# An encoder layer with routed experts: x laid out transposed by the host, router work reordered, one sum in DRAM

## The chip, the core and the metric

The kernel runs on one NeuronCore of a Trainium2 chip. Its engines are TensorE (PE, with PEld for the weight loads), VectorE (DVE), ScalarE (ACT), GpSimd (POOL) and SyncE (SP). SP and ACT issue plain DMAs. POOL issues the DMAs whose rows are named by an index table, and the accumulating ones, from its own queue. The metric is the device time of one execution in microseconds (us); less is better.

## The reference, cut to what matters

1024 tokens of width 1024 go through one layer. The first half is a projection (with a convolution, a pooling and an attention branch), an output projection, a residual sum and a layer norm. The second half sends each token to 8 of 64 experts and to one shared expert:

```python
x = layer_norm(DEEPNORM_ALPHA * x + mix, ln1_g[l], ln1_b[l])
scores = sigmoid((x @ w_router).astype(float32))
_, idx = lax.top_k(scores + router_bias, TOP_K)          # 8 of 64
gates = sel / sum(sel) * ROUTED_SCALE
def expert_block(acc, blk):                               # blocks of 128 rows of one expert
    tok, g, e = blk
    xb = x_pad[tok]
    h = silu(xb @ w_gate[e]) * (xb @ w_up[e])
    return acc.at[tok].add((h @ w_down[e]) * g[:, None]), None
shared = swiglu(xt, w_gate_sh, w_up_sh, w_down_sh)
x = layer_norm(DEEPNORM_ALPHA * x + routed + shared, ln2_g[l], ln2_b[l])
```

All matrix products but a few are made to nearly f32 precision from a high and a low part of both operands, as three products (`PRODS`).

## The kernel before, in words

**Start.** SP loads eight tiles of x, 128 tokens by 1024 channels each, into `xin` (line 370), the first weight block `wraw` after four of them (line 372), then mem and two more weight blocks. PE transposes every x tile (lines 1541 to 1545, the helper at 1536), ACT copies the transposes out of PSUM as the high part of `xT` (line 707), DVE subtracts to get the low part (line 1032). Then come the 20 projection jobs of `JOBS` in their order (line 1546), each with its weight block split by ACT (`split_hi`, line 700) and DVE (`split_lo`, line 1023). `gate0`, the transposes of mem, `a0` and `gate1` are the first on PE (line 1561 for the products). The gated product of `gate0` and `a0` (line 1132) starts the convolution on DVE (lines 1105 and 1109), which runs on through the later jobs.

**In front of the expert loop.** For each tile t of 128 tokens, PE runs the output projection, transposes the normalised tile x1 (line 1710), then runs the shared expert's gate and up products of tile t - 1 (line 1729) and the router logits of tile t (line 1716). DVE routes (line 1258), ranks (line 1236), and POOL scatters the (token, gate) pairs into `list_d`, 8 indirect DMAs per tile (line 598). After the last tile DVE and PE build the tables of work items (lines 1349 and 1769), the shared expert's rows are finished (down products, lines 1829 to 1847), and ACT writes them with plain DMAs into the second half of `sum_d` (`put_shared`, line 919). SP writes x1 into the first half (line 410). When all list scatters have landed, POOL loads the first index tables (line 669) and gathers the rows of the first item (line 639).

**The expert loop.** An item is 128 rows of one expert; there are 96. Per item PE transposes the gathered rows of the next item, transposes the hidden rows of the item before (line 1821), and runs gate and up (line 1790) and the down products of the item before (line 1808). ACT scales the result into `ysb[s]` (`y_out`, line 912) after the scatter that last read that buffer has landed (line 941), copies the high parts, and at an expert's first item also those of the next expert's three weight matrices (lines 899 and 837); DVE makes the low parts. SP streams each expert's three 1 MB matrices into eight slots (`load_expert`, line 434). POOL runs `fetch` in order: gather of an item two ahead (line 639), load of an index table (line 632), then `add_rows` (line 644), an accumulating scatter of a finished item into one of two DRAM sums, chosen by the item's parity, so that neighbouring scatters may be in flight together:

```python
def fetch(q, c):
    gather(q, c + 1)
    if not isinstance(q, int) or q * RING + c - 5 >= NT:
        g.wait_ge(s_yd[(c - 5) % 2], 16 * nth_put(q, c - 5))
    ...
    load_pairs(q, c + 3)
    if not isinstance(q, int) or q * RING + c - 3 >= NT:
        add_rows(q, c - 3)
```

**The end.** SP loads both sums (`load_early`, `load_late`, lines 503 to 516). Tiles 0 and 4 (`ADDED`) are added by DVE (line 1516), the others by PE with an identity matrix (line 1865). ACT takes the moments of six tiles (lines 993 to 1003), DVE those of tiles 0 and 4 (line 1504), POOL the reciprocal root (line 690), DVE normalises every tile in order (lines 1492 to 1499), SP writes it out (line 519).

## Time and profile before

| what | value |
|---|---|
| time, median of 3 runs | 1371.61 us (1370.96 to 1372.6) |
| the profiled execution's own time | 1372.02 us |
| its span, first to last instruction | 1370.4 us |
| mean granted TensorE clock | 0.976 of full speed |
| PE busy, share of the span | 1302.6 us, 95% |
| DVE, ACT, POOL busy | 955.1, 795.3, 486.4 us |

The span is what the trace shows; 1.6 us of the execution's time lie outside it. Rows of the trace give a start and a duration in us from the span's start, the engine, the line of the kernel, and in brackets the idle time ahead of an instruction and what ended it.

### The profile page before, as it was taken

The numbers are of one execution on the slowest core, as the hardware profiler recorded it, in microseconds if no ns is written. First come the engines' busy times: TensorE is split into PE (matmuls) and PEld (weight loads), VectorE is DVE, ScalarE is ACT, GpSimd is POOL, SyncE is SP. The second block draws the span as 40 slices with busy tenths as digits, with TensorE's granted clock in tenths as the row PEclk, the third lists the DMA queues.
The fourth block names the chain that finished last, engine by engine and source line by source line (L and its number), as shares of the span: only waits on it lengthen the run. The fifth ranks groups of instructions, "written<-read, shape, count | busy, mean of one in ns | idle before, by whom it ended". The sixth has DMA issues, their size and how long they took to land.

```text
span 1370.4 us, 25641 instructions
## 1 busy us (share of the span) xinstructions
PE 1302.6 (95%) x6331; PEld 1076.4 (79%) x6332; DVE 955.1 (70%) x1121; ACT 795.3 (58%) x1055; POOL 486.4 (35%) x440
## 2 busy tenths in 40 slices
PE   8989888999988999999999999999999999999966
PEld 6877676788867888888888888888888888788842
DVE  5799986876663968565787366557678679777736
ACT  4122276322344868575796466656678678677724
POOL 0000124366563343343343343334334344443322
PEclk9999989999998999999999999999999999999987
DMA  6022124222468998987999788869889899999657
GB/s 249 31 77 78 62 92 132 93 87 85 136 219 323 329 331 309 325 270 251 332 338 342 235 251 273 260 197 316 277 277 377 250 329 336 339 341 299 191 135 289
DMA packets 78065, 324.11 MB, mean 237 GB/s; under 512 B 22656, under 2 KB 24864, under 8 KB 52816
## 3 DMA queue, kind: packets, MB, share of 16 engines
q1 hardware_dynamic: 43152, 251.05, 48.8%
q0 software_dynamic: 33728, 68.47, 21.4%
q10 hardware_dynamic: 1152, 4.19, 0.8%
q8 instruction: 16, 0.26, 0.1%
q14 instruction: 17, 0.14, 0.0%
HBM read 290.51 MB, written 67.72 MB: 261 GB/s over the span
## 4 chain that ended last, share of the span: by engine, by line
PE 86%; DVE 6%; DMA 3%; issue 2%; ACT 2%; POOL 1%; SPq 0%; POOLq 0%; ACTq 0%; DVEq 0%
PE ps L1790 39%; PE ps L1808 19%; PE ps L1536 7%; PE ps L1657 6%; PE ps L1561 6%; PE ps L1736 2%; DVE cv L1109 2%; PE ps L1821 2%; POOL list_d L598 1%; PE ps L1648 1%; PE ps L1573 1%; DMA xin<-in_x 1%; PE ps L1566 1%; PE ps L1724 1%; DMA late__124<-sum_d 1%
## 5 line engine op out<-in xcount | busy, mean ns | idle before, releaser
L1790 PE MATMUL ps<-wgu,xTe 128*128 x2304 | 548.9, 394 | 2.5 <-ACT wgu L837 1.2
L1790 PEld LDWEIGHTS ps<-wgu,xTe 128*128 128x128 f32 x2304 | 425.7, 188 | 89.3 <-issue 4.3
L649 POOL DMA_INDIRECT sum_d<-ysb,idx x95 | 176.8, 1861 | 510.5 <-ACT ysb L914 403.4
L1808 PE MATMUL ps<-wdn,hT 128*128 (+1 forms) x1236 | 299.5, 391 | 0.0
L1407 DVE TENSOR_TENSOR wgu<-raw,wgu (+1 forms) x128 | 287.7, 2289 | 6.4 <-issue 3.1
L1808 PEld LDWEIGHTS ps<-wdn,hT 128*128 128x128 f32 x1236 | 232.6, 189 | 48.2
L837 ACT CAST wgu<-raw (+1 forms) x128 | 246.9, 1929 | 4.1 <-SPq L448 3.6
L1412 DVE TENSOR_TENSOR xTe<-ps,xTe 128x512 fp32r<-128x512 f32 x194 | 124.6, 684 | 141.9 <-ACT xTe L906 141.9
L914 ACT ACTIVATE ysb<-ps,idx 128x512 f32<-128x512 f32 x188 | 119.3, 686 | 122.3 <-PE ps L1808 122.3
L1407 DVE TENSOR_TENSOR wdn<-raw,wdn x64 | 146.7, 2293 | 59.5 <-ACT wdn L899 59.3
L639 POOL DMA_INDIRECT xg<-x_d,idx x99 | 112.4, 1135 | 44.7 <-issue 35.5
L899 ACT CAST wdn<-raw x64 | 124.9, 1952 | 0.0
L958 ACT ACTIVATE hs<-ps 128x256 f32<-128x256 f32 x96 | 36.9, 384 | 142.2 <-PE ps L1790 142.2
L906 ACT CAST xTe<-ps 128x512 fp32r<-128x512 f32 x194 | 104.3, 598 | 12.1 <-PE ps L1536 11.3
L1536 PE MATMUL ps<-ident,xg 128*128 128x128 f32 x776 | 101.3, 274 | 10.4 <-DMA xg<-x_d,idx 10.4
L1561 PE MATMUL ps<-xT,whl 128*128 128x512 f32 x480 | 110.1, 390 | 0.0
L1536 PEld LDWEIGHTS ps<-ident,xg 128*128 128x128 f32 x776 | 91.0, 141 | 23.4 <-DMA xg<-x_d,idx 10.8
L1561 PEld LDWEIGHTS ps<-xT,whl 128*128 128x128 f32 x480 | 89.9, 188 | 19.2 <-issue 0.4
L1441 DVE TENSOR_TENSOR hx<-hs,ps 128x256 f32<-128x256 f32 x96 | 40.1, 417 | 88.2 <-ACT hs L958 88.1
L598 POOL DMA_INDIRECT list_d<-tg,addr x64 | 76.7, 1199 | 54.9 <-DVEq L1256 38.3
L1657 PE MATMUL ps<-wo,mst 128*128 128x512 f32 x384 | 92.9, 400 | 0.4 <-issue 0.4
L1657 PEld LDWEIGHTS ps<-wo,mst 128*128 128x128 f32 x384 | 72.6, 192 | 15.8 <-issue 0.9
(229 smaller groups left out, 1161.6 us busy)
## 6 DMA issues: line engine op xcount, KB each, us to landing
raw<-in_w_gate SPq DMA_DIRECT2D x64, 1024.0 KB, 11.7
raw<-in_w_up SPq DMA_DIRECT2D x64, 1024.0 KB, 8.8
raw<-in_w_down SPq DMA_DIRECT2D x64, 1024.0 KB, 9.7
wraw<-in_w_in SPq DMA_DIRECT2D x10, 512.0 KB, 3.4
xin<-in_x SPq DMA_DIRECT2D x8, 512.0 KB, 7.8
wraw<-in_w_kv SPq DMA_DIRECT2D x8, 512.0 KB, 3.3
wor<-in_w_out SPq DMA_DIRECT2D x4, 1024.0 KB, 8.6
xres<-in_x SPq DMA_DIRECT2D x8, 512.0 KB, 4.5
```

The source lines that it names most:

```text
L639: g.indirect_dma_start(out=xg[:, c % 2], out_offset=None, in_=x1_d, in_offset=bass.IndirectOffsetOnAxis(ap=idx[:, c % RING, 0:1], axis=0), ...
L649: g.indirect_dma_start(out=sums, out_offset=bass.IndirectOffsetOnAxis(ap=idx[:, c % RING, c % 2:c % 2 + 1], axis=0), in_=ysb[:, c % 2], in ...
L837: nc.scalar.copy(wgu[:, v, 0, :, n * XD:(n + 1) * XD].rearrange("p a c n -> p (a c) n"), raw[:, bass.ds(slot_of(e, n), 1)].rearrange("p a ...
L899: nc.scalar.copy(wdn[:, v, 0].rearrange("p a c n -> p (a c) n"), raw[:, bass.ds(slot_of(e, 2), 1)].rearrange("p a (c n) -> p (a c) n", c=2 ...
L914: nc.scalar.activation(dst[:, b * 512:(b + 1) * 512], ps[:, bank + b, :], ACT.Copy, scale=scale).then_inc(s_y, 1)
L1407: V.tensor_tensor(dst, raw_, hi.bitcast(F), ALU.subtract).then_inc(done, 1)
L1412: last = V.tensor_tensor(xTe[:, s, 1, 4 * b:4 * b + 4], ps[:, b, :].rearrange("p (c n) -> p c n", c=4), xTe[:, s, 0, 4 * b:4 * b + 4].bitc ...
L1536: last = nc.tensor.transpose(ps[:, bank + c // 4, (c % 4) * 128:(c % 4 + 1) * 128], src[:, c * 128:(c + 1) * 128], ident[:])
L1561: last = mm(ps[:, b + h, :], wt[:, st, d], xT[:, mo, d, h * 512:(h + 1) * 512], start=(d == 0 and st == 0 and mo == 0), stop=(d == ND - 1 ...
L1657: last = mm(ps[:, project_bank(t, h), :], mixed(t)[:, st, c], wo[:, mo, c, h * 512:(h + 1) * 512], start=(first and c == blocks[0] and st ...
L1790: last = mm(ps[:, 2 + s, :], xTe[:, s, st, d], wgu[:, w, mo, d].rearrange("p a n -> p (a n)"), start=(d == 0 and st == 0 and mo == 0), sto ...
L1808: last = mm(ps[:, down_bank(i) + h, :], hT[:, s, st, c], wdn[:, w, mo, c, h * 512:(h + 1) * 512].rearrange("p a n -> p (a n)"), start=(c = ...
```

## The change

- The host also lays x out transposed (`xt`: two halves of 512 tokens, each in four pieces of 128 partitions by 1024). The kernel loads these pieces, ACT and DVE split them straight from SBUF, the 64 PE transposes go, and PE runs `gate0` and `a0` half by half. The transposes of mem follow behind `a0`.
- In front of the loop, logits move between two parts of the shared expert's products (`BEFORE`: after 4 of 8 blocks, at the last tile after 7), DVE routes before it multiplies the shared hidden rows, and the rank product of tile 6 moves ahead of the transposes of tile 7. The item tables are made by one matmul with a ones matrix over diagonals that DVE builds (`tdiag`).
- There is one `sum_d`. x1 is written into it, POOL adds the shared rows with accumulating DMAs (`add_shared`) in place of ACT's plain writes, and every expert scatter goes to it. Each scatter waits until the one ahead has landed. ACT waits for the adds of shared tiles 2 to 5 before it overwrites their SBUF rows with an expert's weights. SP holds expert 2's second load until the list scatters have landed (`s_seen`).
- At the end each tile of the one sum is loaded and used directly.

```diff
+BEFORE = (4,) * (NT - 1) + (7,)
-        sum_d = nc.dram_tensor("sum_d", [2, S, D], F, kind="Internal").ap()
+        sum_d = nc.dram_tensor("sum_d", [S, D], F, kind="Internal").ap()
# SP
-            for t in range(NT):
-                sp.dma_start(xin[:, t], a["x"][t]).then_inc(s_x[t], 16)
-                if t == 3:
-                    project_weights(0)
+            for h in range(2):
+                project_weights(h)
+                for c in range(4):
+                    sp.dma_start(xin[:, h, c], a["xt"][h, c]).then_inc(s_x[4 * h + c], 16)
+            project_weights(2)
...
                 if e0 == 2:
                     landed(e0, 0, rounds)
+                    sp.wait_ge(s_seen, 1)
...
             for t in range(NT):
-                if t >= 2:
-                    load_early(t, s_late[t])
-                load_late(t)
+                sp.dma_start(late_[:, t], sum_d[t * 128:(t + 1) * 128, :]).then_inc(s_late[t], 16)
# POOL
+            def add_shared(j):
+                g.wait_ge(s_y, 2 * j + 4)
+                landed = s_ysf if j < 2 else s_ysh
+                g.dma_start(sum_d[j * 128:(j + 1) * 128, :], shared_rows(j), accum_op=ALU.add).then_inc(landed[j % 2], 16)
+            add_shared(0)
+            add_shared(1)
             g.wait_ge(s_tabs, 1)
...
                 g.wait_ge(s_y, 2 * (q * RING + c) + 4)
+                if not isinstance(q, int) or q * RING + c > NT:
+                    g.wait_ge(s_yd[(c - 1) % 2], 16 * nth_put(q, c - 1))
...
             for r in range(RING):
                 fetch(1, r)
+                if r == 0:
+                    for j in range(2, NT - 2):
+                        add_shared(j)
+                elif r < 3:
+                    add_shared(NT - 3 + r)
# ACT
+            for h in range(2):
+                split_hi(h)
+                for c in range(4):
+                    act.wait_ge(s_x[4 * h + c], 16)
+                    nc.scalar.copy(xT[:, 0, 2 * c:2 * c + 2, h * 512:(h + 1) * 512],
+                                   xin[:, h, c].rearrange("p (a n) -> p a n", a=2)).then_inc(s_xhi, 1)
...
+                scores_of(t)
                 if t >= 1:
                     shared_silu(t - 1)
-                scores_of(t)
...
-                put_shared(u)
...
                 nxt = act.value_load(tab[0:1, 1, bass.ds(i, 1)], min_val=0, max_val=NE)
+                if known and i == NT:
+                    for parity in range(2):
+                        act.wait_ge(s_ysh[parity], 16 * 2)
# DVE
+            for h in range(2):
+                split_lo(h)
+                for c in range(4):
+                    v.wait_ge(s_xhi, 4 * h + c + 1)
...
+            route(NT - 1)
             shared_hidden(NT - 2)
-            route(NT - 1)
...
+                for b, n in ((0, 128), (1, TAB - 128)):
+                    step(V.tensor_tensor(tdiag[:, :, b * 128:b * 128 + n], ...
...
-            add(0)
             moments(0)
# PE
+            for h in range(2):
+                for j in range(2):
+                    if h == 0:
+                        pe.wait_ge(s_wlo, j + 1)
+                    for d in range(ND):
+                        if j == 0 and d % 2 == 0:
+                            pe.wait_ge(s_xlo, 4 * h + d // 2 + 1)
+                        for st, mo in PRODS:
+                            last = mm(ps[:, result(j) + h, :], whl[:, j, st, d], xT[:, mo, d, h * 512:(h + 1) * 512], ...
...
+                if t == NT - 1:
+                    ranks(t - 1)
                 x1_transposed(t)
+                if t >= 1:
+                    shared_gate_up(t - 1, range(BEFORE[t]))
                 if t == NT - 1:
                     hidden_transposed(0)
-                    ranks(t - 1)
+                logits(t)
                 if t >= 1:
-                    shared_gate_up(t - 1)
-                logits(t)
+                    shared_gate_up(t - 1, range(BEFORE[t], ND))
...
-            pe.wait_ge(s_early, 32)
-            add_part(1, early)
-            for t in summed:
...
-                add_part(t, late_).then_inc(s_pc, 1)
```

## Rows read from the trace of the kernel before

**Rows 1.** The page: the chain that ended last, by engine.
```profile
PE 86%; DVE 6%; DMA 3%; issue 2%; ACT 2%; POOL 1%; SPq 0%; POOLq 0%; ACTq 0%; DVEq 0%
```
**Rows 2.** Stretches: PE, PEld, DVE, ACT, POOL busy us; granted clock, DMA share, GB/s.
```profile
416.80:444.00 27.20, 27.14 (x129) 22.98 (x130) 12.46 (x14) 14.56 (x22) 6.20 (x7) 0.91 0.96 375
600.00:1100.00 500.00, 499.98 (x2476) 419.94 (x2475) 326.45 (x315) 336.03 (x423) 190.63 (x161) 1.00 0.88 285
1100.00:1292.00 192.00, 189.36 (x929) 157.81 (x929) 145.07 (x128) 141.38 (x166) 75.90 (x62) 1.00 0.94 316
```
**Rows 3.** The page's groups: line, engine, op, count, busy us, mean ns, idle before.
```profile
L899 ACT CAST wdn<-raw x64 | 124.9, 1952 | 0.0
L958 ACT ACTIVATE hs<-ps 128x256 f32<-128x256 f32 x96 | 36.9, 384 | 142.2 <-PE ps L1790 142.2
```
**Rows 4.** The chain in order of time (start us, us, what), 0 to 200 us.
```profile
16.91 10.93 PE ps L1561 x48
29.60 21.78 PE ps L1561 x96
```
**Rows 5.** The timeline of the start.
```profile
15.82 1.09 PE L1536 MATMUL ps<-ident,xin 128*128 128x128 f32 x8 [0.19 <-DMA xin<-in_x]
40.52 1.23 DVE L1132 TENSOR_TENSOR glu<-ps,glu 128x1024 f32<-128x1024 f32 x1 [9.13 <-PE ps L1561]
40.60 1.05 ACT L700 CAST whl<-wraw 128x1024 fp32r<-128x1024 f32 x1 [10.47 <-PE ps L1561]
```
**Rows 6.** The timeline in front of the loop.
```profile
373.23 1.93 ACT L892 CAST wdn<-wdnr 128x2048 fp32r<-128x2048 f32 x1
381.62 0.29 DVE L1261 TENSOR_REDUCE sb__96<-ps 128x64 f32<-128x128 f32 x1
416.86 1.97 PE L1536 MATMUL ps<-ident,xg 128*128 128x128 f32 x8 [10.39 <-DMA xg<-x_d,idx]
```
**Rows 7.** The chain in order of time, 200 to 430 us.
```profile
400.44 6.25 DMA list_d<-tg,addr
```
**Rows 8.** The timeline of the loop's first items.
```profile
419.68 1.03 POOL L639 DMA_INDIRECT xg<-x_d,idx  x1 [4.50 <-issue]
425.90 1.91 ACT L899 CAST wdn<-raw  x1
430.53 0.41 DVE L1441 TENSOR_TENSOR hx<-hs,ps 128x256 f32<-128x256 f32 x1
432.96 0.38 PE L1821 MATMUL ps<-ident,hx 128*128 128x128 f32 x2
```
**Rows 9.** All instructions of line 649, the scatters: the last row of that view.
```profile
DMA to landing us min/median/max: 4.6/10.3/12.3
```
**Rows 10.** The chain in order of time, 600 to 620 us: two items' first gate and up products.
```profile
600.91 5.47 PE ps L1790 x24
...
610.20 5.47 PE ps L1790 x24
```
**Rows 11.** DMA issues (count, KB, median us to landing): 583 to 585, 592.5 to 594.5, 440 to 560.
```profile
sum_d<-ysb,idx POOLq DMA_INDIRECT x1, 6.2
...
sum_d<-ysb,idx POOLq DMA_INDIRECT x1, 10.8
...
sum_d<-ysb,idx POOLq DMA_INDIRECT x13, 10.8
```
**Rows 12.** The timeline of the end.
```profile
1333.11 1.23 DVE L1516 TENSOR_TENSOR acc<-early,late__124 128x1024 f32<-128x1024 f32 x1 [11.95 <-DMA late__124<-sum_d]
1334.37 1.29 DVE L1504 BATCH_NORM_STATS2 stat<-acc 128x6 f32<-128x512 f32 x2
1336.01 1.27 DVE L1492 SCALAR_TENSOR_TENSOR acc<-acc,mv,g 128x1024 f32<-128x1024 f32 x1
1342.42 1.28 DVE L1496 SCALAR_TENSOR_TENSOR acc<-ps,lnst,g 128x1024 f32<-128x1024 f32 x1 [3.24 <-POOL rs L690]
1366.09 1.28 DVE L1499 SCALAR_TENSOR_TENSOR acc<-acc,rs,b 128x1024 f32<-128x1024 f32 x1
```

More of the change, by code:

```diff
@@ L409, in _ @@
                 sp.wait_ge(s_x1, t + 1)
-                for rows in (x1_d, xa_d):
+                for rows in (x1_d, sum_d):
                     sp.dma_start(rows[t * 128:(t + 1) * 128, :], xres[:, t % 2]).then_inc(s_x1w[t % 2], 16)
@@ L713, in _ @@
                     split_hi(17)
-                elif w in W_JOBS and W_JOBS.index(w) < 16:
+                elif w in W_JOBS and 0 < W_JOBS.index(w) < 16:
                     split_hi(W_JOBS.index(w) + 1)
@@ L940, in step_act @@
                 shared = known and i - 2 < NT
[L941 removed]
+                if known and i < NT + 2:
+                    act.wait_ge(s_ysf[s], 16)
+                elif known:
+                    act.wait_ge(s_ysh[s], 16 * (NT // 2 - 1))
+                else:
+                    act.wait_ge(s_yd[s], 16 * nth)
                 act.wait_ge(s_dn, i - 1)
                 y_out(ysb[:, s], 1.0 / ALPHA if shared else idx[:, bass.ds((i - 2) % RING, 1), 2:3].bitcast(F).rearrange("p a n -> p (a n)"))
[L944 to L945 removed]
                 item_hi(i + 1, 1 - s)
@@ L1096, in _ @@
                 both = ps[:, b:b + 2, :].rearrange("p a n -> p (a n)")
-                if w in W_JOBS and W_JOBS.index(w) < 17:
+                if w in W_JOBS and 0 < W_JOBS.index(w) < 17:
                     split_lo(W_JOBS.index(w) + 1)
@@ L1540, in _ @@
             pe.wait_ge(s_iden, 1)
-            for t in range(NT):
-                pe.wait_ge(s_x[t], 16)
-                if t >= 4:
-                    pe.wait_ge(s_xlo, max(u for u in range(t) if XBANKS[u] == XBANKS[t]) + 1)
-                transpose_tile(xin[:, t], 2 * XBANKS[t]).then_inc(s_xt, 1)
+            for h in range(2):
[6 more added lines that the diff above has]
+                        for st, mo in PRODS:
+                            last = mm(ps[:, result(j) + h, :], whl[:, j, st, d], xT[:, mo, d, h * 512:(h + 1) * 512],
+                                      start=(d == 0 and st == 0 and mo == 0), stop=(d == ND - 1 and st == 1))
+                    if h == 1:
+                        last.then_inc(s_job, 1)
+            for m in range(2):
+                pe.wait_ge(s_mln, m + 1)
+                transpose_tile(memin[:, m], 2 * m).then_inc(s_mt, 1)
             for j, w in enumerate(JOBS):
+                if j < 2:
+                    continue
                 b = result(j)
@@ L1582, in _ @@
                 last.then_inc(s_job, 1)
-                if w == "gate0":
-                    for m in range(2):
-                        pe.wait_ge(s_mln, m + 1)
-                        transpose_tile(memin[:, m], 2 * m).then_inc(s_mt, 1)
             def conv_mean():
@@ L1733, in shared_gate_up @@
                     pe.wait_ge(s_h, u - 1)
-                for d in range(ND):
+                for d in blocks:
                     for st, mo in PRODS:
@@ L1737, in shared_gate_up @@
                                   start=(d == 0 and st == 0 and mo == 0), stop=(d == ND - 1 and st == 1))
-                last.then_inc(s_gu, 1)
+                if blocks[-1] == ND - 1:
+                    last.then_inc(s_gu, 1)
             def hidden_transposed(u):
@@ L1771, in item_tables @@
                 pe.wait_ge(s_cm, 1)
-                for f in range(3):
-                    for b, n in ((0, 128), (1, TAB - 128)):
-                        last = mm(ps[0:1, 7, f * TAB + b * 128:f * TAB + b * 128 + n], tabf[:, f, b:b + 1],
-                                  ident[:, 0:n], start=True, stop=True)
-                last.then_inc(s_tabp, 1)
+                pe.wait_ge(s_pt2, 9)
+                mm(ps[:, 7, 0:3 * TAB], onef[:], tdiag[:].rearrange("p a n -> p (a n)"),
+                   start=True, stop=True).then_inc(s_tabp, 1)
             def rows_transposed(s):
@@ L1860, in _ @@
             pe.sem_inc(s_endC, 1)
-            pe.wait_ge(s_endC, 3)
-            def add_part(t, rows):
-                for h in range(2):
-                    last = mm(ps[:, 2 * (t % 4) + h, :], ident[:], rows[:, t, h * 512:(h + 1) * 512],
-                              start=(rows is early), stop=(rows is late_))
-                return last
-            summed = [t for t in range(NT) if t not in ADDED]
-            pe.wait_ge(s_early, 32)
-            add_part(1, early)
-            for t in summed:
-                pe.wait_ge(s_late[t], 16 if t < 2 else 32)
-                if t >= 4:
-                    pe.wait_ge(s_acc, t - 3)
-                if t >= 2:
-                    add_part(t, early)
-                add_part(t, late_).then_inc(s_pc, 1)
 def pool_edges():
```

106 lines of the change are left out of this document (30 added, 76 removed).

## The prediction, made before the changed kernel had run

> **What bounds the kernel now.** I read the page's chain first: PE carries 86% of it, DVE 6%, DMA 3% [rows 1]. So most of the time can only change where PE waits. Next the busy time by stretch: from 600 to 1100 us PE is busy for 499.98 of 500.00 us, so no other engine sets the pace there; late in the loop it is busy for 189.36 of 192.00, with the DMA engines 0.94 occupied [rows 2]. The loop has 96 items, and 64 of them bring in a new expert's weights [rows 3]; an item without them leaves the DMA engines time to recover. From 600 to 1100 us that nets out at a share of 0.88. The change edits four places, so I read those four: the start, the front of the loop, the loop's scatters, the end. The loop's products stay as they are.
>
> **1. The start.** `gate0`'s 48 products take 10.93 us from 16.91 on, 0.228 us each; `a0` and `gate1` follow at 29.60 and take 21.78 together [rows 4]. DVE's gated product starts at 40.52, when `a0` ends [rows 5], and `gate1` ends at 51.38 (29.60 + 21.78). From there the convolution on DVE carries the chain, so what PE and DVE both reach earlier, the stage ends earlier. The last transposes take 1.09 us after a wait of 0.19 for their tile, so tiles land 1.28 us apart, the eighth just ahead of 15.82. With two weight blocks among the eight pieces instead of one, the last piece lands at about 15.8 + 1.28 = 17.1. A split of 128x1024 costs ACT 1.05 and DVE 1.23 [rows 5], less than two landings, on engines that do nothing else then. The fourth piece of the first half is the fifth load and lands five spacings earlier, at 10.7; split at 13.0, and its last 6 products end at 14.3. Then three half jobs of 24 products, 5.47 us each, run on behind each other: `a0`'s first half to 19.8, `gate0`'s second (its last piece is split at 19.4) to 25.3, `a0`'s second to 30.7. The transposes of mem, moved behind `a0`, take 1.75 (29.60 less the end of `gate0`, 16.91 + 10.93 = 27.84), and `gate1` ends at 30.7 + 1.75 + 10.9 = 43.4 instead of 51.4: **-8.0 us**. Ends: -10 (DVE's taps start 9.8 earlier), -3 if the first 24 products ran at half clock while PE waits for pieces between them (24 x 0.228 = 5.5 more).
>
> **2. The front of the loop.** For tiles 1 to 6 the order changes and the work doesn't; PE stays busy, so nothing. At tile 7 the hidden transposes stand behind 7 blocks of the shared products, so ACT's copy of `wdn`, at 373.23 now, starts only some 5.5 us later, and DVE, which needs it before it routes tile 7, routes about 1.4 us after 381.62 [rows 6]. The scatters of tile 7 then start about 1.4 us later; those of tile 6 a few tenths earlier. The landing of the last list scatter (6.25 us after 400.44 [rows 7]) gets shorter, since SP now holds the 1 MB load that was in flight. But POOL puts two accumulating adds of 512 KB into its queue ahead of the index loads. The extra two DVE products and the one matmul of the tables end well before the scatters land. PE starts the loop at 416.86, having waited 10.39 us for the gather [rows 6], so what this chain gains or loses goes through: **+1.5 us**, between -1 (the shorter landing alone) and +4 (both adds ahead of the index loads).
>
> **3. The loop's first items.** POOL issues four adds of 512 KB behind the second gather. It idled for 4.50 us ahead of its third gather at 419.68 [rows 8], so the issues cost little; the queue is what matters. The third gather stands behind the adds, and ACT waits for all four before its copies at 425.90, with the copies, the silu behind them and PE's use of the hidden rows at 432.96 queued behind that wait [rows 8]. DVE's product behind the silu ends at 430.94 (430.53 + 0.41), so about 2.0 us are room. No row shows a plain accumulating DMA. Lower end: a 512 KB tile lands every 1.28 us at the start [rows 5]; an add reads and writes, so about 2.6 us each (an estimate), four from about 417 to 427: nothing is late. Upper end: the weights, which keep the share at 0.96 here [rows 2], take half of the engines, the adds land at 437 and 437 - 425.9 - 2.0 - 1.5 is 8 us, and some 3 us more for the later gathers: +11. Nearer to the upper row, as the share is so high, yet the adds go in ahead of the next experts' loads: **+5 us**.
>
> **4. The hold in the loop.** A scatter lands 10.3 us after its issue in the median, 4.6 at best [rows 9]; two items' first products stand 9.29 us apart (610.20 - 600.91) [rows 10]. So every second scatter is held, and behind it on POOL the next gather and index load, and behind the gather PE. If each kept its latency, the 64 items with weights would add 10.8 + 0.1 - 9.3 = 1.6 us each (102 us) and the 32 others, at 6.2, would give back up to 3.0 each (96 us) [rows 3, 11]: between +6 and +102 less a few us of room, by how the two kinds alternate. If on the other hand the landing is set by the work queued in the DMA engines, a later issue lands at the same time: 0. For this speaks that holding adds no bytes and that the queue never grows: 13 scatters in a row, issued faster than they landed, still have a median of 10.8 [rows 11]. Against it, the scatter issued near 593 took 10.8 although the one before, issued near 584 with 6.2, was long down [rows 11]: weights in flight, not the scatter ahead, make it slow. But when PE slows, the weights are asked for more slowly too, and the wait shrinks. I take the queue as the cause for most of it: **+2.5 us**, ends 0 and, short of rival B, +13. The Trainium skill's page "DMA: Bandwidth & Descriptors" (Anatomy of one DMA) puts a DMA of this queue at about 2.0 us plus bytes over 436 GB/s, an estimate of 3.2 us for 512 KB; by that the hold would cost nothing at all. The traced 10.3 differs: the page's DMA is alone.
>
> **5. The end.** Now DVE adds at 1333.11, takes moments at 1334.37 (1.64 to the next step at 1336.01) and starts its last operation at 1366.09, ending at 1367.37; its normalisations wait for ACT, which waits for PE's additions [rows 12]. After the change the first tile is used as it lands, at 1333.1. Half as many bytes follow it, and no PE step. DVE is then the limit: two moments of 1.64, eight normalisations of 2 x 1.28 plus 0.16 between, 2.72 each, together 25.0: done at 1358.1. That is -9.2; with a small wait, **-9.0 us**; ends -10.5 and -7 (ACT's moments in the way).
>
> **The sum** is -8.0 + 1.5 + 5.0 + 2.5 - 9.0 = -8.0 against the profiled execution's 1372.0, which is 0.4 above the median shown: 1364.0.
>
> **The rivals.** *A, the hold and the adds are free:* -8 + 1.5 - 9 = -15.5, 1356.5; the 4.50 us of POOL idle and the lower ends speak for it, the share of 0.96 against. *B, the held scatters pace the loop:* latencies stay, halfway between +6 and +102 is +54, so 1364 - 2.5 + 54 = 1415.5; it decides once a scatter issued after its hold still needs more than 9.2 us. The scatter near 593 speaks for it, the constant 10.8 against; a partial form gives +20, 1381.5. This is the slower side. *C, a jam at the loop's first items* eats the whole gain: 3 and 4 give +15.5 together, 1372, no change. The same skill page (Queues, rings and completion order) says that each DMA engine round-robins between queues by packets; by that the adds would share with the weights, which leans to C; no row here separates the two queues. *D, the start isn't gained:* -3 instead of -8, 1369.
>
> **Chances.** The forecast 0.42, A 0.18, B with its partial form 0.17, C 0.15, D 0.08. About 0.2%, 2.7 us, is what a measurement of this kernel can tell from no change. Faster: the forecast, A, and three quarters of D, 0.66. Same: two thirds of C and the rest of D, 0.12. Slower: B and the rest of C, 0.22. The likeliest case alone spans 1358 to 1369. The range reaches over A with its own low ends to 1352, and over C and B's partial form to 1388; the full B stays outside.
>
> **What would show it.** Right: `gate1` ends near 43 us; the loop's first transposes start near 410 (416.9 - 8 + 1.5); ACT waits for a DMA ahead of its first `wdn` copy; items still take 9.3 us in the middle although POOL's idle time ahead of scatters is ended by DMAs; the end is some 32 us from the last landing to the last instruction. Wrong: items of 10.5 us or more in runs of new experts, with PE idle until a gather lands (B); a gap of 10 us or more behind the first item (C).

## The result, and the profile after

The changed kernel takes 1443.18 us in the median of its runs (1435.04 to 1457.83) against 1372.11 for the kernel before beside it: a ratio of **1.0492, interval 1.0459 to 1.0525**: 68 us slower by the ratio (0.0492 x 1372.11), 71 between the medians. The profiled execution, of 1457.83 us and a span of 1456.2, is the one slow run of the four, so the terms read in it below say where the time goes, and where the size matters it is checked on the experiments, whose profiles are all of fast runs.

The page after, its chain by engine and by line:

```profile
PE 55%; DMA 25%; issue 7%; DVE 7%; ACT 2%; POOL 1%; POOLq 1%; ACTq 0%; DVEq 0%; SPq 0%
PE ps L1785 22%; DMA sum_d<-ysb,idx 14%; DMA xg<-x_d,idx 10%; PE ps L1803 10%; PE ps L1650 5%; PE ps L1522 4%; PE ps L1558 4%; PE ps L1729 2%; PE ps L1536 2%; DVE cv L1101 2%; PE ps L1816 1%; PE ps L1641 1%; PE ps L1570 1%; POOL list_d L578 1%; PE ps L1614 1%
```

PE carried 86% of the chain before [rows 1] and carries 55% now. The DMA share went from 3% to 25%, and 14% of the chain is one transfer alone, the scatter of expert rows into the sum. A bound that has changed its engine is read from this line before anything else.

The same three stretches as in [rows 2], after (PE, PEld, DVE, ACT, POOL busy, granted clock, DMA share, GB/s):

```profile
416.80:444.00 27.20, 15.23 (x69) 12.67 (x69) 5.14 (x7) 8.04 (x11) 5.48 (x7) 0.75 0.99 299
600.00:1100.00 500.00, 473.89 (x2292) 392.03 (x2291) 299.22 (x289) 308.74 (x389) 196.25 (x151) 0.99 0.80 261
1100.00:1292.00 192.00, 177.19 (x835) 145.69 (x834) 131.13 (x115) 130.69 (x153) 76.81 (x56) 0.96 0.88 298
```

PE now idles in each of the three stretches, and from 600 us on the DMA engines are less busy than before: 0.80 in the middle where they had 0.88. So behind the first items no engine and no bandwidth has become the bound; something waits for something in turn. The page's groups after say what (columns as in [rows 3]):

```profile
L1785 PE MATMUL ps<-wgu,xTe 128*128 x2304 | 567.1, 403 | 25.9 <-issue 21.9
L642 POOL DMA_INDIRECT sum_d<-ysb,idx x95 | 185.1, 1948 | 553.5 <-DMA sum_d<-ysb,idx 310.2
L897 ACT CAST wdn<-raw x64 | 124.2, 1940 | 17.6 <-DMA sum_d<-ysh 15.5
```

Of the 553.5 us that POOL idles ahead of its scatters, 310.2 end with the landing of the scatter ahead. The view of the kernel before's scatters has 403.4 us end with ACT's `ysb` there (us, times), which is work that has not been done yet and costs nothing; the view of PE's waits after (us in total, times, longest) shows what the hold does to PE:

```profile
  ACT ysb L914: 403.4, 76
```

```profile
PE ps L1522 <- DMA xg<-x_d,idx: 51.2, 22, 12.0
```

PE waits 22 times for gathered rows, 51.2 us in all; before it did so once, for 10.4 us, ahead of the first item [rows 6]. POOL's timeline in a stretch of new experts shows the cycle:

```profile
703.64 1.62 POOL L642 DMA_INDIRECT sum_d<-ysb,idx  x1 [6.39 <-DMA sum_d<-ysb,idx]
705.57 2.82 POOL L630 DMA_INDIRECT xg<-x_d,idx  x1 [0.30 <-issue]
708.40 0.60 POOL L623 DMA_DIRECT2D idx<-list_d  x1
714.81 1.63 POOL L642 DMA_INDIRECT sum_d<-ysb,idx  x1 [5.81 <-DMA sum_d<-ysb,idx]
716.74 1.04 POOL L630 DMA_INDIRECT xg<-x_d,idx  x1 [0.30 <-issue]
717.79 0.60 POOL L623 DMA_DIRECT2D idx<-list_d  x1
725.93 1.62 POOL L642 DMA_INDIRECT sum_d<-ysb,idx  x1 [7.54 <-DMA sum_d<-ysb,idx]
```

The scatters stand 11.17 and 11.12 us apart, where an item takes 9.29 [rows 10]. The cycle is one landing plus 0.87 us until POOL issues the next scatter: in the chain of waits the scatter of 703.64 lands 10.29 us after its issue, and 703.64 + 10.29 + 0.88 is 714.81. The next gather and index load are issued behind the held scatter, so while the holds last PE gets its rows at the same pace.

The parts of the +85.8 us between the two spans, from marks in the two traces. The start, in the timeline after:

```profile
8.02 24.54 PE L1536 MATMUL ps<-xT,whl 128*128 128x512 f32 x96 [8.02 <-DVE xT L1026]
34.06 16.13 PE L1558 MATMUL ps<-xT,whl 128*128 128x512 f32 x70
45.24 1.03 ACT L722 ACTIVATE glu<-ps 128x1024 f32<-128x1024 f32 x1 [11.52 <-PE ps L1558]
```

ACT's sigmoid behind `gate1` starts at 45.24 instead of 51.40: 6.2 us earlier. In front of the loop and at its first items, the chain in order of time after:

```profile
402.41 8.05 DMA idx<-list_d
411.40 4.44 DMA xg<-x_d,idx
...
418.72 23.88 DMA xg<-x_d,idx
```

and the timeline there:

```profile
415.88 1.97 PE L1522 MATMUL ps<-ident,xg 128*128 128x128 f32 x8 [10.92 <-DMA xg<-x_d,idx]
439.36 1.90 ACT L897 CAST wdn<-raw  x1 [15.46 <-DMA sum_d<-ysh]
442.73 1.96 PE L1522 MATMUL ps<-ident,xg 128*128 128x128 f32 x8 [11.97 <-DMA xg<-x_d,idx]
444.49 0.66 PE L1816 MATMUL ps<-ident,hx 128*128 128x128 f32 x2
```

The loop begins at 415.88 against 416.86 [rows 6], 1.0 us earlier, so 5.2 of the start's 6.2 are gone. From there to the hidden rows' transposes it takes 28.61 us; before it took 16.10 (416.86 to 432.96, [rows 6, 8]): **+12.5**. ACT waited 15.46 us for the adds of the shared rows, and the third gather, behind the same adds, took 23.88 us to land. The last scatter's landing and the end, the chain after and the same row of the kernel before:

```profile
1416.51 6.07 DMA sum_d<-ysb,idx
1423.32 4.36 DMA late__125<-sum_d
...
1451.87 1.29 DVE acc L1494
```

```profile
1323.03 6.18 DMA sum_d<-ysb,idx
```

From the hidden rows' transposes to the last landing it is 444.49 to 1422.58, 978.1 us, against 432.96 to 1329.21, 896.3: **+81.8**. From the last landing to the end of the span it is 33.6 us against 41.2: -7.6. The sum is -1.0 + 12.5 + 81.8 - 7.6 = 85.7. The profiled execution is 14.7 us over the median; with the other three terms as they are, the 71.1 between the medians leave 67.2 for the loop instead of 81.8.

### The profile page after: what moved, and what is told of

Same layout as the page of the kernel before. It is cut to its first block, busy times and chain, and to the rows that moved or that the text cites. A ratio compares the mean times of both kernels' runs of the same rounds, so it can differ in the third digit from the quotient of the medians.

```text
span 1456.2 us, 25334 instructions
## 1 busy us (share of the span) xinstructions
PE 1299.8 (89%) x6209; PEld 1073.9 (74%) x6210; DVE 953.7 (65%) x1113; ACT 795.1 (55%) x1045; POOL 532.0 (37%) x449
## 4 chain that ended last, share of the span: by engine, by line
PE 55%; DMA 25%; issue 7%; DVE 7%; ACT 2%; POOL 1%; POOLq 1%; ACTq 0%; DVEq 0%; SPq 0%
PE ps L1785 22%; DMA sum_d<-ysb,idx 14%; DMA xg<-x_d,idx 10%; PE ps L1803 10%; PE ps L1650 5%; PE ps L1522 4%; PE ps L1558 4%; PE ps L1729 2%; PE ps L1536 2%; DVE cv L1101 2%; PE ps L1816 1%; PE ps L1641 1%; PE ps L1570 1%; POOL list_d L578 1%; PE ps L1614 1%
## 5 line engine op out<-in xcount | busy, mean ns | idle before, releaser
L1785 PE MATMUL ps<-wgu,xTe 128*128 x2304 | 567.1, 403 | 25.9 <-issue 21.9
L1785 PEld LDWEIGHTS ps<-wgu,xTe 128*128 128x128 f32 x2304 | 439.1, 194 | 123.1 <-issue 33.6
L642 POOL DMA_INDIRECT sum_d<-ysb,idx x95 | 185.1, 1948 | 553.5 <-DMA sum_d<-ysb,idx 310.2
L630 POOL DMA_INDIRECT xg<-x_d,idx x99 | 141.5, 1429 | 36.2 <-issue 30.3
L1522 PE MATMUL ps<-ident,xg 128*128 128x128 f32 x776 | 104.4, 279 | 51.2 <-DMA xg<-x_d,idx 51.2
L1558 PE MATMUL ps<-xT,whl 128*128 128x512 f32 x384 | 88.1, 390 | 0.0
L1558 PEld LDWEIGHTS ps<-xT,whl 128*128 128x128 f32 x384 | 71.9, 188 | 15.5 <-issue 0.4
```

The source lines that it names most:

```text
L630: g.indirect_dma_start(out=xg[:, c % 2], out_offset=None, in_=x1_d, in_offset=bass.IndirectOffsetOnAxis(ap=idx[:, c % RING, 0:1], axis=0), ...
L642: g.indirect_dma_start(out=sum_d, out_offset=bass.IndirectOffsetOnAxis(ap=idx[:, c % RING, 0:1], axis=0), in_=ysb[:, c % 2], in_offset=Non ...
L1522: last = nc.tensor.transpose(ps[:, bank + c // 4, (c % 4) * 128:(c % 4 + 1) * 128], src[:, c * 128:(c + 1) * 128], ident[:])
L1558: last = mm(ps[:, b + h, :], wt[:, st, d], xT[:, mo, d, h * 512:(h + 1) * 512], start=(d == 0 and st == 0 and mo == 0), stop=(d == ND - 1 ...
L1785: last = mm(ps[:, 2 + s, :], xTe[:, s, st, d], wgu[:, w, mo, d].rearrange("p a n -> p (a n)"), start=(d == 0 and st == 0 and mo == 0), sto ...
```

## The experiments

Theories, in short: **H**, a held scatter still takes as long as it took when it was not held, and a held one plus 0.87 us is longer than an item; against it **Q**, the step of the prediction, by which holding moves nothing since the landing is set by what is queued. Landing times below that stand in no view are counted from each transfer's issue and landing in the trace; "slow" landings are those over 8 us.

**e1, the hold alone,** on the kernel before, with its two sums:

```diff
                 g.wait_ge(s_y, 2 * (q * RING + c) + 4)
+                if not isinstance(q, int) or q * RING + c > NT:
+                    g.wait_ge(s_yd[(c - 1) % 2], 16 * nth_put(q, c - 1))
```

> The kernel before with the hold alone: two sums, all else as before, each scatter waits for the one ahead. Theory H (a held scatter still needs its own 10.4 us while weights are in flight, so the item takes that plus 0.87 us instead of 9.29): the loop loses what the changed kernel's loop lost, 66 us at its median run (80 in its profiled one, which was 14 us above the median), so about 1438 us, 1425 to 1455. Rival Q (the step of the prediction: the landing is set by what is queued, holding costs 0 to 13 us, and the changed kernel lost its time to the single sum, whose rows follow each other on the same bytes): 1372 to 1385 us. In the trace H expects some 50 held scatters with a median landing of 10 us or more; Q expects landings that shrink by as much as the scatter was held.

Measured: 1443.4 us against 1373.63, ratio 1.0502 (1.0481 to 1.0524), +69.8 us. Two lines of wait alone cost as much as the whole change. The view of its scatters (what ended POOL's idle time ahead of them, us and times):

```profile
  DMA sum_d<-ysb,idx: 322.8, 53
```

H holds in its time, Q falls, and so does the single sum as a cause: here neighbouring scatters go to different tensors. Of the 95 scatters 57 were slow, 10.06 us in the mean; in the kernel before 67 were, with 10.55. The cut at 8 us leaves out those that became quick, so here are all of them too: the mean fell from 9.32 to 8.55 us and the median from 10.3 to 9.1. That is some 73 us over the 95. The 53 were issued 4.0 us in the mean after ACT had written them, 3.1 more than the 0.93 of the kernel before: some 161 us of hold. Q wanted all of it back in shorter landings, and under half came. The 53 themselves landed in 9.1 us in the median, not in the 10 or more that H had expected; the landings that they had to wait for took 9.6 (median).

What the hold takes away is overlap. In the kernel before 58 scatters were issued while the one ahead was still in flight; here none is.

**e2, no adds of shared rows:** `add_shared` and all waits on `s_ysf` and `s_ysh` are taken out of the changed kernel.

```diff
-            add_shared(0)
-            add_shared(1)
...
-                if r == 0:
-                    for j in range(2, NT - 2):
-                        add_shared(j)
...
-                if known and i == NT:
-                    for parity in range(2):
-                        act.wait_ge(s_ysh[parity], 16 * 2)
```

> The changed kernel without the adds of the shared expert's rows (left out of the output) and without the waits on them. The changed kernel's third gather landed 23.9 us after its issue behind these adds and the second item's products started 13.1 us later than before. Theory J (that jam is lost time for good): 1443 - 13 = 1430 us, and the second item's products within 10 us of the first's. Rival (the jam fills buffers ahead, weights and tables, and the held scatters would have taken most of it anyway): 1438 to 1443 us.

Measured: 1426.52 us, ratio 1.0404 (1.0362 to 1.0446), 16.7 less than the changed kernel's 1443.18 between the medians, 12 by the two ratios (0.0088 x 1373). Theory J holds: the jam is lost for good. Its timeline in front of the loop:

```profile
412.51 1.97 PE L1504 MATMUL ps<-ident,xg 128*128 128x128 f32 x8 [4.92 <-DMA xg<-x_d,idx]
```

Without the two adds ahead of the index loads the loop begins at 412.51, 3.4 us earlier than in the changed kernel; with that taken off, 9 to 13 us are left for the first items (12.5 in the trace). That the adds ate the start's gain doesn't follow: e3 and e7, which have ACT's plain writes in their place and one and the same front, begin their loops at 416.09 and 411.89, so the profiled executions differ by as much.

**e3, start and front with two sums:** the kernel before with `xt`, `BEFORE`, the new order and the new tables; scatters, shared rows and end as before.

```diff
+BEFORE = (4,) * (NT - 1) + (7,)
...
-            for t in range(NT):
-                sp.dma_start(xin[:, t], a["x"][t]).then_inc(s_x[t], 16)
+            for h in range(2):
+                project_weights(h)
...
+            route(NT - 1)
             shared_hidden(NT - 2)
-            route(NT - 1)
```

> The kernel before with the new start, the new order in front of the loop and the new item tables; two sums, scatters, shared rows and end as before. The changed kernel began its loop 1.0 us earlier than before although its gate1 ended 6.2 us earlier. Theory F (the order in front of the loop gives back 5 us by itself): 1371 us, 1369 to 1372. Rival (the give-back is the work of POOL's two adds and of the index loads behind them, which landed 8.1 us after issue instead of 3.7): without them the loop begins 4 to 5 us earlier and the time is 1366 us, 1364.5 to 1367.5.

Measured: 1369.09 us, ratio 0.9943 (0.9917 to 0.9968). Not decided: the median is at F's lower end, the ratio (1365.8 us) in the rival's range; its runs lie at 1360.84 and 1362.34 and from 1368.46 to 1371.2. The profiled one (1371.2) begins its loop at 416.09, behind an index load of 6.04 us and a gather, although no POOL add stood ahead: ACT's plain writes of the shared rows are in flight there. Whether the two quickest runs began it earlier no profile shows.

**e4, weights by half** from the fourth expert on, with hold, adds and single sum as changed:

```diff
+            def half_load(e, n, slot):
+                sp.dma_start(raw[:, slot, 0:1024],
+                             a[MATRIX[n]][bass.ds(e - 1, 1)].rearrange("a p n -> (a p) n")[:, 0:1024]).then_inc(
+                    s_raw[slot], 16)
```

> The changed kernel, but from the fourth expert on each matrix is loaded by half (columns 0 to 1023 of 2048; the other half of the slot keeps older weights, so the output is not the reference's). Theory H with its price set by the weights in flight: held scatters land in 6 to 8 us, under 9.29 with 0.87 added, the loop falls back to 9.3 us per item and the time to 1443 - 66 = 1377 us, 1370 to 1390. Rival (the 10.4 us belong to a held accumulating scatter as such, by its descriptors and its reads and writes of DRAM): landings stay over 9.5 us and the time over 1425 us.

Measured: 1372.82 us, ratio 0.9994 (0.9977 to 1.001). The stretch 450 to 1290 us of this kernel, and of e1 (columns as above):

```profile
450.00:1290.00 840.00, 840.00 (x4157) 705.67 (x4156) 581.45 (x542) 593.00 (x722) 317.36 (x271) 1.00 0.72 189
```

```profile
450.00:1290.00 840.00, 799.70 (x3843) 661.82 (x3842) 541.74 (x503) 549.92 (x670) 320.34 (x252) 0.98 0.85 281
```

With half the weights PE is busy for all of the 840 us though the wait is still there. The scatter itself is unchanged in rows and bytes; its slow landings (37 of them) fell to 8.55 us, 7.2 in the median of all, and 8.55 + 0.87 is about an item. So the price of the hold is set by the weights in flight, as H had it. Loading half of the columns also shortens the weights' rows, from 8 KB to 4; e10 has rows of 2 KB with all the bytes, and its slow landings stay at 9.25 us, so the bytes count beside the rows.

**e5, the sum in two column halves,** so that two scatters of 256 KB may be in flight:

```diff
-                if not isinstance(q, int) or q * RING + c > NT:
-                    g.wait_ge(s_yd[(c - 1) % 2], 16 * nth_put(q, c - 1))
+                for h, landed in enumerate((s_yd, s_ye)):
+                    if not isinstance(q, int) or q * RING + c > NT:
+                        g.wait_ge(landed[(c - 1) % 2], 16 * nth_put(q, c - 1))
...
+                        in_=ysb[:, c % 2, cols(h)], in_offset=None, compute_op=ALU.add,
```

> The changed kernel with its one sum cut by columns into two tensors of 1024 x 512: every scatter becomes two of 256 KB, each held until the same half of the item ahead has landed, so that two transfers can be in flight. Theory N (what costs is that only one scatter is in flight, and a scatter's landing with weights in flight is mostly time in the queue, about 10 us whatever its size): halves issued one behind the other land nearly together, about 10 us after issue, and nothing is gained: 1435 to 1450 us. Rival S (a landing scales with the bytes: with the weights halved it fell from 10.3 to 8.55 us): halves land in 7 to 8.4 us, less than 9.29 - 0.87, the holds cost little, 1380 to 1395 us with the jam of the first items still in it.

Measured: 1470.75 us, ratio 1.0707 (1.0679 to 1.0735): slower still, and over N's range too. Of the 190 halves, 106 were slow, 10.13 us in the mean, so S falls. Of N the landing of about 10 us is there and its picture is not: behind a slow first half the second lands 3.1 us later (median of 58), and from the first half's issue to the second's landing it is 11.0 us (median of 95), where the changed kernel's whole scatter takes 8.8. N also did not count that POOL now issues two scatters an item and is held twice. How much of the loss is which isn't separated:

```profile
L651 POOL DMA_INDIRECT sum_d<-ysb,idx x190 | 360.1, 1895 | 381.7 <-DMA sum_d<-ysb,idx 216.7
```

**e6, the start alone** on the kernel before (the part of the diff that touches `xt`, `xin` and the first jobs).

```diff
+                    for d in range(ND):
+                        if j == 0 and d % 2 == 0:
+                            pe.wait_ge(s_xlo, 4 * h + d // 2 + 1)
```

> The kernel before with the new start alone (transposed x, gate0 and a0 by halves). In the changed kernel gate1 ended 6.2 us earlier, and the last output projection 3.5 us earlier, ahead of the loop. Theory F1 (part of the start is given back by the stages behind it, the rest goes through): loop and time 3 to 5 us earlier, 1368.5 to 1370.5 us against 1373.6. Rival F2 (the index loads and the first gather ahead of the loop wait for bytes in flight, not for PE): the loop begins within 1 us of where it did, 1372.5 to 1374.5 us.

Measured: 1366.58 us, ratio **0.9957 (0.9942 to 0.9971)**, 5.9 us (0.0043 x 1372.6). Its loop begins 4.1 us earlier than before:

```profile
412.74 1.97 PE L1529 MATMUL ps<-ident,xg 128*128 128x128 f32 x8 [11.81 <-DMA xg<-x_d,idx]
```

F1 holds in kind, with 5.9 us where it had 3 to 5. It beats both kernels, and e3's interval overlaps its own: the new order in front of the loop adds nothing that these runs show.

**e7, all loads of the earlier sum ahead of the last landing,** on e3:

```diff
-            for t in range(2):
-                load_early(t, s_early)
+            for t in range(NT):
+                load_early(t, s_early if t < 2 else s_late[t])
```

> The new start and front with two sums, as in the experiment e3, and all eight loads of the earlier sum asked for before the last scatter has landed, not two of them. The changed kernel's end took 33.6 us from the last landing, e3's 38.6. Theory E (the end waits for bytes: 16 tiles behind the last landing): 8 tiles fewer behind it, 3 to 5 us off, 1364 to 1366 us. Rival (the early loads stand in the last scatter's way, or DVE's normalisations are the limit there): 1368 to 1371 us.

Measured: 1371.83 us, ratio 0.9993 (0.9981 to 1.0005): E falls, and the time lies 0.8 us over the rival's range. In its chain the last scatter takes 9.88 us where e3's takes 6.05; the one thing that is new beside it is the loads of the earlier sum, 4 MB:

```profile
1318.47 9.88 DMA sum_d<-ysb,idx
```

**e8, e3 without SP's wait** for the list scatters (one line taken out):

```diff
-                    sp.wait_ge(s_seen, 1)
```

> The experiment e3 without SP's wait that holds expert 2's second matrix until the list scatters have landed. e3's profiled run lost some 10 us around 1128 to 1198 us waiting for weights and for a gather. Theory W (weights held back at the front are late all through the loop): without the wait the stall goes, 1361 to 1365 us. Rival (the stall belongs to a stretch of single-block experts, where 3 MB come every 9.3 us, whatever happened at the front; the earlier weights only slow the index loads): 1369 to 1372 us, with the loop beginning up to 2 us later.

Measured: 1369.65 us, ratio 0.9971 (0.9952 to 0.999). It lies in the rival's range and is not told apart from e3: W is not shown, and the wait is worth nothing that can be measured. There was little to win: e3's PE is busy for 67.66 of the 70 us from 1128 to 1198, the kernel before's for 68.64.

**e9, one weight load in flight:**

```diff
                 load(e, 0, slot_of(e0, 0))
+                if e0 >= 4:
+                    landed(e0, 0, rounds)
```

and the same behind the second matrix and ahead of the first.

> The changed kernel with SP asking for an expert's matrix only when the one ahead of it has landed, from the fourth expert on: the same bytes, one load of 1 MB in flight instead of up to three or more. A held scatter, a 256 KB half and even a 1.5 KB index load took 8 to 10 us while weights were in flight, so the landing is time spent behind the weights. Theory D (it is the depth: a POOL transfer stands behind all weights asked for ahead of it): held scatters land in 6 to 8 us. Rival R (it is a sharing by turns, whatever the depth): with one load in flight they still land in 9.5 to 10.5 us. The total says little, since one load at a time may be too slow for the stretches of single-block experts.

Measured: 1651.43 us, ratio 1.2026 (1.1966 to 1.2086): PE is short of work, since ACT waits 285.3 us for weights. But 80 of the 95 scatters take under 8 us, and the median of all is 7.3 where it was 8.8 in the changed kernel. The DMA view of 450 to 1290 us (KB each, median us from issue to landing) shows that weights were in flight most of the time even so, three loads of 5 to 7 us for each expert (the third is left out below):

```profile
raw<-in_w_down SPq DMA_DIRECT2D x45, 1024.0 KB, 4.9
raw<-in_w_gate SPq DMA_DIRECT2D x45, 1024.0 KB, 7.2
...
sum_d<-ysb,idx POOLq DMA_INDIRECT x71, 7.3
```

The landings are in D's range, not in R's. But the loop is longer, so the bytes come more slowly too (229 GB/s over this stretch, 273 in the changed kernel). That it is the depth and not the rate isn't shown.

**e10, weight rows of 2 KB** in place of 8 KB, on the changed kernel:

```diff
-                sp.dma_start(raw[:, slot], a[MATRIX[n]][bass.ds(e - 1, 1)].rearrange("a p n -> (a p) n")).then_inc(
-                    s_raw[slot], 16)
+                for k in range(4):
+                    cols = slice(k * 512, (k + 1) * 512)
+                    sp.dma_start(raw[:, slot, cols], a[MATRIX[n]][bass.ds(e - 1, 1)].rearrange("a p n -> (a p) n")[:, cols]).then_inc(
+                        s_raw[slot], 16)
```

> The changed kernel with each weight matrix loaded as four transfers of 512 columns (rows of 2 KB where they were 8 KB): the same bytes in flight, in shorter pieces. Theory R (POOL's transfers and the weights take turns by the piece, so a long weight row holds each of the scatter's pieces up): held scatters land in 6 to 8 us and the time falls below 1420 us. Theory D (by the bytes queued ahead): landings stay at 9.5 to 10.5 us and the time at 1435 to 1460 us.

Measured: 1399.4 us (1392.76 and 1406.04), ratio 1.0191 (1.0073 to 1.0308): 44 us less than the changed kernel for the same bytes. The slow landings fell from 10.40 to 9.25 us, a half way that neither theory had; 9.25 + 0.87 is 0.8 us over an item's 9.29, where 10.40 + 0.87 was 2.0 over. The length of the weights' rows matters beside their bytes; how the two share the 10.4 us is left open.

**e11, weight rows of 1 KB,** the same with eight transfers:

```diff
+                for k in range(8):
+                    cols = slice(k * 256, (k + 1) * 256)
```

> The changed kernel with each weight matrix loaded as eight transfers of 256 columns (rows of 1 KB). With rows of 2 KB held slow scatters landed in 9.25 us instead of 10.40 and the time fell by 44 us to 1399. Theory R (taking turns by the piece): the landing falls on, to 8.4 us or less, the holds end under an item's 9.29 us and the time is 1375 to 1390 us, the first items' jam of some 14 us still in it. Rival D2 (the fall with 2 KB rows was the smaller step in which the weights are asked for, or the rest of the landing is the bytes ahead): landings stay near 9.2 us, 1395 to 1405 us; or the short rows cost the weights their rate and PE waits for them: over 1405 us.

Measured: 1426.89 us, ratio 1.0398 (1.0374 to 1.0422). The slow landings go on falling, to 8.83, in R's direction and short of its 8.4, but the last rival decides the time. PE's waits in this run (us in total, times, longest), and from 450 to 1290 us ACT's wait for SP's word that weights have landed, and the windows view:

```profile
PE ps L1818 <- DVE hx L1440: 23.1, 11, 3.8
PE ps L1787 <- ACT wgu L837: 19.0, 16, 1.4
PE ps L1524 <- DMA xg<-x_d,idx: 9.5, 2, 9.1
```

```profile
ACT wgu L837 <- SPq L451: 72.9, 16, 6.8
```

```profile
450.00:1290.00 840.00, 802.95 (x3862) 667.58 (x3860) 541.72 (x504) 546.10 (x671) 335.71 (x252) 0.98 0.97 281
```

Only 2 waits for a gather are left of 22. PE waits for ACT's and DVE's work instead, and ACT waited 72.9 us for weights from 450 to 1290, which it did not in the changed kernel; the DMA engines are at 0.97.

**e12, the new start with 2 KB weight rows,** two sums, no hold (the edits of e6 and e10 on the kernel before):

```diff
+                    cols = slice(k * 512, (k + 1) * 512)
```

> The kernel before with the new start and the 2 KB weight rows, two sums and no hold: a candidate to beat both kernels. The new start alone was at 0.9957 of before, 1366.6 us. Theory R+ (index loads and gathers come earlier, so the last small waits of PE in the stretch of single-block experts and ahead of the loop go): 1361 to 1365 us. Rival (PE hides these landings when no scatter is held, and the shorter rows change nothing that PE waits for): 1365.5 to 1368 us.

Measured: 1369.03 us, ratio 0.9979 (0.9965 to 0.9993), over the rival's range and not better than e6's 0.9957. Its slow landings are 9.20 us against e6's 10.52: the shorter rows do here what they did in e10. Where no scatter is held, PE hides the landings and the short rows buy nothing. e6 is the version to keep.

Not tried: a single sum without the hold, with two scatters in flight to the same rows. Whether the sums would come out right is shown by no run, so what the single sum would be worth with two transfers in flight stays unknown. Nor were the gathers asked for further ahead, so that PE's rows would not stand behind a held scatter.

## Why the prediction was wrong, point by point

- **What bounds the kernel** was right: PE, to within 0.02 us of 500 in the middle of the loop. That is also why the hold was so costly: whatever PE waits for is lost.
- **1, the start, -8.0.** `gate1` came 6.2 us earlier, within the ends, and e6 measures 5.9 for it. The term that was off is the stream of 96 products: they began at 8.02 as pieces landed and took 24.54 us to 32.56, where the prediction had them done at 30.7. That "the stage ends earlier" by as much was wrong: the last output projections before and after show 3.5 us left of the 6.2.

```profile
L1657 PE MATMUL ps<-wo,mst x384: 387/389/774, 211.8 to 362.6; 128*128 128x512 f32 x192
```

```profile
L1650 PE MATMUL ps<-wo,mst x384: 387/389/774, 206.9 to 359.1; 128*128 128x512 f32 x192
```

- **2, the front of the loop, +1.5.** Measured: from there to the loop's start another 2.5 us went, within the ends. The mechanism named for the upper end, the two adds ahead of the index loads, is there (the index load lands at 410.46, right behind the second add's 410.28), but the plain writes in e3 delay the loop as much, so what the adds themselves cost isn't shown.
- **3, the first items, +5, ends 0 to +11.** Right in mechanism (the adds behind the weights, ACT's wait for all four), too small in size: 12.5 in the trace, 9 to 13 by e2. The adds landed at about 439, as the upper end had said (437), and the third gather behind them cost the rest. That "the adds go in ahead of the next experts' loads" was the reason for not taking that end, and it did not count.
- **4, the hold, +2.5: the step that failed.** The words were "I take the queue as the cause for most of it", that is, a scatter issued later would land at the same time. e1 measured +69.8: under half of the hold came back in shorter landings, and in the changed kernel's stretch of new experts the scatters came 11.1 us apart where an item takes 9.29. The evidence read for the queue (13 scatters in a row with a median of 10.8 [rows 11]) shows only that a landing is constant; it fits a constant price just as well. The evidence against it, the scatter near 593 [rows 11], was read rightly ("weights in flight, not the scatter ahead, make it slow") and then outvoted.
- A row of the kernel before that the prediction did not read looks as if it would have settled it: the DMA view of 440 to 1290 us has a load of 1.5 KB that takes as long as 512 KB.

```profile
sum_d<-ysb,idx POOLq DMA_INDIRECT x91, 10.5
xg<-x_d,idx POOLq DMA_INDIRECT x91, 11.2
idx<-list_d POOLq DMA_DIRECT2D x91, 1.5 KB, 10.2
```

  It settles nothing. In this trace POOL's transfers land in the order of their issue (none of 257 from 450 us on lands ahead of the one issued before it), and the index load lands 0.2 to 1.0 us behind the gather issued just ahead of it, in all 70 cases where both are recorded. Its 10.2 us are the gather's. What bears on the hold is a scatter with nothing of POOL's in flight ahead of it, so that no queue of POOL's own can explain its landing. The kernel before has 19 that are known to be so: their median is 9.2 us, and 13 of them took over 8. That is the scatter near 593 again, many times over. Where a POOL transfer is still in flight ahead, the scatter lands 5.0 us behind it (median of 51), and 6.4 in e1 (median of 75): transfers of the one queue overlap, and the hold takes part of that away.
- **Rival B was the outcome**, by its own condition: a scatter issued after its hold that needs more than 9.2 us (the landings that the changed kernel's 49 holds waited for took 10.3 in the median). Its price, +54, was the middle of +6 and +102, and that low end rested on a give-back that the runs don't show: "the 32 others, at 6.2, would give back up to 3.0 each". In e1 PE never took less than 9.27 us from one item's first gate and up products to the next's. What short landings can do is refill the room that the gather's lead allows. In e1's trace the landings plus 0.87 exceed 9.29 us by 94.7 us in sum, over 53 scatters, close to the prediction's 102; PE's items exceed 9.29 by 68.0. That leaves about 27 us for the room. Between the medians the loop lost 69.8 us (e1) and 67.2 (the changed kernel).
- **5, the end, -9.0.** Right: -7.6, within its ends. DVE has the last word, as forecast: from the first moments at 1426.21 to the end of the last operation, 1453.16, it is 26.95 us, where 25.0 were worked out. The look from the last landing to the end, "some 32 us", was 33.6.
- **The page's sum.** The Trainium skill's page "DMA: Bandwidth & Descriptors" (Anatomy of one DMA) gave an estimate of 3.2 us for 512 KB of this queue. The quickest scatter after took 5.0 us, those over 8 us 10.40 in the mean, and the halves of 256 KB over 8 us 10.13 (e5): for a transfer beside weights in flight the page's sum does not hold. The same page (Queues, rings and completion order) has an engine take turns between queues by whole packets. The fall with shorter weight rows, 10.40, 9.25, 8.83 us (e10, e11), would agree with it if a shorter row makes a shorter turn, which no run here shows.

The range, 1352 to 1388, left the full B out. With the 19 scatters read, B would have weighed more than its 0.17.

## What to carry to other kernels

In this PE-bound loop two scatters could be in flight, and landings of 10 us and more cost nothing at 9.29 us an item. A wait that allows only one leaves each an item's time less the issue; what lands later is lost but for the room ahead of PE, and short landings win nothing beyond refilling that room. Before serialising transfers, look in the trace for those that had nothing of their own queue ahead of them: their landing time beside the other traffic, plus the issue, is what to hold against the item's time. A small load issued behind a large one on the same queue is no guide, since here it landed right behind the large one. Merging the two accumulation targets saved bytes once, at the end (7.6 us here), and the wait that came with it cost the second transfer in flight at every item (about 70).

## What the runs showed that was not expected

- **A stall can cost twice.** After some of the waits for a gather PE's next products run slowly. The chain after, around one such wait:

```profile
506.03 11.82 DMA xg<-x_d,idx
...
521.01 7.79 PE ps L1785 x24
...
532.61 5.49 PE ps L1785 x24
```

  The 24 products take 7.79 us instead of 5.49. The windows view gives the granted clock of 518 to 530 us as 0.72, a mean between the half level (1.2 GHz) and the full one (2.4); before it PE had stood still for 1.97 us, waiting for gathered rows. Not every wait does it: one of 2.03 us ahead of 505.52 was followed by 24 products in 5.75 us, at a granted clock of 1.00. Over the loop the gate and up products take 567.1 us after and 562.8 in e1, against 548.9 in the kernel before (the group of line 1790 there): in e1 13.9 us of the loss are slower products, not waiting. In e4, without stalls, they take 551.2.
- **Plain accumulating DMAs beside weights come in one by one.** The four adds of 512 KB issued from 414.36 on held ACT until 439.36; they landed at 422.65, 429.43, 433.86 and 438.89, so each took 4.4 to 6.8 us behind the one ahead. The medians from issue to landing in the DMA view of the page after hold that queueing:

```profile
sum_d<-ysb POOLq DMA_DIRECT2D x4, 512.0 KB, 10.4
sum_d<-ysh POOLq DMA_DIRECT2D x4, 512.0 KB, 16.4
```

- **Shorter rows for the bulk loads help the other queue** (10.40 to 9.25 us at 2 KB, for the same bytes), until the loads themselves become late (1 KB: DMA engines at 0.97, ACT waiting 72.9 us for weights).
